# Softmax rows of three attentions: divided by their sums on GpSimd instead of on VectorE

## The reference

```python
x += W_out[ groupnorm(FoX heads) | groupnorm(MLA heads) | groupnorm(dilated-window heads) ]
x += memory cross-attention(rmsnorm(x), rmsnorm(mem))   # 4 heads, 256 memory tokens
x += top-4-of-32 clamped-SwiGLU experts(rmsnorm(x))
```

```python
p = jax.nn.softmax(s, axis=-1)      # exp(s - max) divided by its row sum
out = einsum("bhqk,bkhd->bqhd", p, v)
```

## Time and profile before

| what | value |
|---|---|
| median of 3 runs | 1135.68 us (1135.57 to 1135.76) |
| the profiled execution's own time | 1137.97 us |
| its span, first to last instruction | 1136.2 us |
| TensorE busy | 1091.2 us (96%) |
| VectorE busy | 316.2 us (28%) |
| ScalarE busy | 192.3 us (17%) |
| GpSimd busy | 136.2 us (12%) |
| mean DMA rate over the span | 378 GB/s |

### The profile page before, as it was taken

One profiled execution on the slowest core, in us unless ns is written; L12 is line 12 of the kernel. 1 busy time (PEld: TensorE's weight loads), 2 busy tenths in 40 slices (PEclk: granted clock), 3 DMA queues, 4 the chain that ended last, 5 costly groups with the idle time before them and its releaser, 6 DMA issues.

```text
span 1136.2 us, 13637 instructions
## 1 busy us (share of the span) xinstructions
PE 1091.2 (96%) x5069; PEld 442.7 (39%) x5069; DVE 316.2 (28%) x666; ACT 192.3 (17%) x389; POOL 136.2 (12%) x289
## 2 busy tenths in 40 slices
PE   7999999999999999999999999999999999999997
PEld 4666756633333333333333333333333333333332
DVE  4475754512222222222222222211211112222222
ACT  1144433311111111111111111111111111110111
POOL 1041300211111111111111111111111111111100
PEclk9999999899999999999999999999999999999999
DMA  6913368399999999999999999999999999999995
GB/s 228 358 38 149 126 241 333 153 389 428 426 429 427 427 429 429 427 430 427 429 427 430 428 427 430 427 429 427 430 428 427 431 427 429 427 430 427 428 430 239
DMA packets 44024, 429.06 MB, mean 378 GB/s; under 512 B 6336, under 2 KB 13792, under 8 KB 19168
## 3 DMA queue, kind: packets, MB, share of 16 engines
q1 hardware_dynamic: 43376, 427.67, 89.8%
q10 hardware_dynamic: 624, 1.07, 0.2%
HBM read 427.67 MB, written 1.05 MB: 377 GB/s over the span
## 4 chain that ended last, share of the span: by engine, by line
PE 66%; DMA 28%; DVE 4%; ACT 1%; issue 1%; ACTq 0%; DVEq 0%; SPq 0%
PE banks L705 27%; DMA ring<-in_w_e_dram 27%; PE banks L725 13%; PE banks L313 8%; PE banks L648 4%; PE banks L675 4%; PE banks L738 2%; PE banks L656 2%; PE banks L295 1%; PE banks L388 1%; PE banks L528 1%; PE banks L664 1%; DMA gain_rows<-in_g_ffn_dram 1%; PE banks L330 1%; PE banks L346 0%
## 5 line engine op out<-in xcount | busy, mean ns | idle before, releaser
L705 PE MATMUL banks<-ring,xg_T 128*64 128x512 f32 x2048 | 478.3, 599 | 24.4 <-DMA ring<-in_w_e_dram 23.2
L705 PEld LDWEIGHTS banks<-ring,xg_T 128*64 128x64 f32 x2048 | 135.8, 136 | 306.1 <-issue 254.3
L725 PE MATMUL banks<-ring,act_T 128*64 128x512 f32 x1024 | 232.9, 596 | 0.4 <-DVE act_T L1826 0.4
L1798 DVE TENSOR_TENSOR x_sb<-x_sb,banks 128x1024 f32<-128x1024 f32 x64 | 78.2, 1221 | 415.2 <-PE banks L675 382.6
L725 PEld LDWEIGHTS banks<-ring,act_T 128*64 128x64 f32 x1024 | 70.3, 137 | 132.5 <-issue 128.1
L1808 DVE TENSOR_TENSOR glu<-banks,b_T 128x512 f32<-128x512 f32 x32 | 22.1, 692 | 242.1 <-PE banks L738 242.1
L1033 POOL COPY picked<-slot_table 128x2 f32 (+1 forms) x32 | 6.0, 188 | 562.9 <-PE banks L664 562.9
L675 PE MATMUL banks<-y_sb,hot_gate_T 64*128 64x512 f32 x256 | 72.0, 640 | 0.8 <-ACT y_sb L1316 0.8
L1303 ACT COPY hidden<-banks 128x1024 f32<-128x1024 f32 x32 | 32.4, 1012 | 206.6 <-PE banks L705 206.6
L1289 ACT COPY xg_rows<-banks 128x512 f32<-128x512 f32 x33 | 19.3, 585 | 272.9 <-PE banks L648 272.9
L648 PE MATMUL banks<-h_sb,hot_slot 128*64 128x512 f32 x264 | 64.1, 607 | 0.5 <-DVE hot_slot L1766 0.5
(11 more groups left out here) (304 smaller groups left out, 777.5 us busy)
## 6 DMA issues: line engine op xcount, KB each, us to landing
ring<-in_w_e_dram SPq DMA_DIRECT2D x190, 2048.0 KB, 37.6
w_out_sb<-in_w_out_dram SPq DMA_DIRECT2D x1, 4096.0 KB, 13.3
ring<-in_w_e_dram SPq DMA_DIRECT2D x4, 1024.0 KB, 40.8
w_in_qk<-in_w_in_dram SPq DMA_DIRECT2D x1, 2048.0 KB, 14.8
w_mkv_sb<-in_w_mkv_dram SPq DMA_DIRECT2D x1, 2048.0 KB, 10.7
w_in_cq<-in_w_in_dram SPq DMA_DIRECT2D x2, 768.0 KB, 7.7
w_in_qc<-in_w_in_dram SPq DMA_DIRECT2D x1, 1536.0 KB, 17.0
w_in_kc<-in_w_in_dram SPq DMA_DIRECT2D x1, 1536.0 KB, 15.2
```

The source lines that it names most:

```text
L705: ins = TE.matmul(PS[SLOTS * h:SLOTS * h + SLOTS, B_W1 + b, :], left, ring[slot][:, 2 * F * j + F * h + 512 * b:2 * F * j + F * h + 512 * ...
L725: ins = TE.matmul(PS[SLOTS * h:SLOTS * h + SLOTS, B_W2, :], actT[:, c % 4, c // 4, :], ring[slot][:, D * j + 512 * h:D * j + 512 * h + 512 ...
L1798: V.tensor_tensor(X[:, t, :], X[:, t, :], PS[:, first:first + 2, :].rearrange("p b n -> p (b n)"), ALU.add).then_inc(S("added"), 1)
```

## The change

The multiplication of the probabilities moves from VectorE's list to GpSimd's. VectorE keeps the reciprocals (`invert_sums`) and counts a new semaphore `sums_inverted`, once for each unit. From the third unit on it waits first until the unit two before it has been scaled, since the reciprocals' columns are used again. GpSimd's `scale_probs` waits for the reciprocals and multiplies; it is called at six places of its list. TensorE's wait on `p_scaled` stays as it is.

```diff
         pool.wait_ge(S("rope_tables"), 1)
+        def scale_probs(*names):
+
+            for name in names:
+                u = U_OF[name]
+                c = 2 * (u % 2)
+                pool.wait_ge(S("sums_inverted"), u + 1)
+                G.tensor_scalar(Pb[:, u % 2, 0:P], Pb[:, u % 2, 0:P], rowinv[:, c:c + 1], None, ALU.mult)
+                G.tensor_scalar(Pb[:, u % 2, P:], Pb[:, u % 2, P:], rowinv[:, c + 1:c + 2], None,
+                                ALU.mult).then_inc(S("p_scaled"), 1)
+
...
         link(G.tensor_tensor(keys, keys, SG["g_kb"].unsqueeze(1).to_broadcast([P, 12, QK]), ALU.mult))
+        scale_probs("f0", "f1")
         for w in (1, 0):
             if w == 0:
+                scale_probs("f2", "f3")
                 pool.wait_ge(S("mla_q_normed"), 1)
...
+        scale_probs("m0", "m1", "m2", "m3")
         pool.wait_ge(S("dil_normed"), 1)
         pool.wait_ge(S("mla_rotated"), 1)
...
+        scale_probs("m4", "m5")
         pool.wait_ge(S("turned_out"), turned_no["gains"])
         pool.wait_ge(S("w_mq_in"), 16)
...
+        scale_probs("d0", "d1", "d2", "d3", "d4", "d5")
         pool.wait_ge(S("router_in"), 16)
...
-        def scale_probs(name):
+        def invert_sums(name):
             u = U_OF[name]
             c = 2 * (u % 2)
             dve.wait_ge(S("exped"), u + 1)
-            link(V.reciprocal(rowinv[:, c:c + 2], rowsum[:, 2 * (u % 4):2 * (u % 4) + 2]))
-            V.tensor_scalar(Pb[:, u % 2, 0:P], Pb[:, u % 2, 0:P], rowinv[:, c:c + 1], None, ALU.mult)
-            V.tensor_scalar(Pb[:, u % 2, P:], Pb[:, u % 2, P:], rowinv[:, c + 1:c + 2], None,
-                            ALU.mult).then_inc(S("p_scaled"), 1)
+            if u >= 2:
+                dve.wait_ge(S("p_scaled"), u - 1)
+            V.reciprocal(rowinv[:, c:c + 2], rowsum[:, 2 * (u % 4):2 * (u % 4) + 2]).then_inc(S("sums_inverted"), 1)
...
```

More of the change, by code:

```diff
@@ L1595, in _ @@
         gain_heads(QKb[:, 0], SG["g_qb"], MLA_H, QK).then_inc(S("mla_q_normed"), 1)
-        scale_probs("f0")
-        scale_probs("f1")
+        invert_sums("f0")
+        invert_sums("f1")
         project("qc", 1)
@@ L1608, in _ @@
         values(0)
-        scale_probs("f2")
-        scale_probs("f3")
+        invert_sums("f2")
+        invert_sums("f3")
         project("kc", 1)
@@ L1618, in _ @@
                   cols_of(0, "dil").rearrange("p (t h) -> p t h", t=NT))
-        scale_probs("m0")
-        scale_probs("m1")
+        invert_sums("m0")
+        invert_sums("m1")
         project("vc", 0)
@@ L1626, in _ @@
         scale_heads(dil, y, 12, HD)
-        scale_probs("m2")
-        scale_probs("m3")
+        invert_sums("m2")
+        invert_sums("m3")
         gain_heads(dil[:, :, 0:6], SG["g_qc"], 6, HD)
@@ L1634, in _ @@
         score("m5")
-        scale_probs("m4")
-        scale_probs("m5")
+        invert_sums("m4")
+        invert_sums("m5")
         group_roots("f", 256)
@@ L1652, in _ @@
         score("d1")
-        scale_probs("d0")
-        scale_probs("d1")
+        invert_sums("d0")
+        invert_sums("d1")
         memory("mem_v", 0, 256)
@@ L1660, in _ @@
         gain_heads(kv, gk[:], MEM_H, HD).then_inc(S("mem_keys_normed"), 1)
-        scale_probs("d2")
-        scale_probs("d3")
+        invert_sums("d2")
+        invert_sums("d3")
         memory("mem_v", 1, 256)
@@ L1667, in _ @@
         score("d5")
-        scale_probs("d4")
-        scale_probs("d5")
+        invert_sums("d4")
+        invert_sums("d5")
         add_group("f", 1, 0)
```

## The result

The changed kernel took **1150.6 us** (median of four runs, 1149.5 to 1152.8) against 1135.7 us for the kernel before in the same session. The ratio is 1.0118, with a 95% interval of 1.0101 to 1.0135, so the change costs **13.4 us** (11.5 to 15.3); the two medians lie 14.9 us apart. The forecast was 1141.9 us, 6.2 over before, with a range of 1136.0 to 1149.5: the sign was right, the size was less than half of what came, and the measured time lies above the range.

What follows compares the result with a forecast made beforehand. The weight stream bounds the expert stage, so attention losses reach the end whole: 2.4 + 1.4 + 1.0 + 1.4 = 6.2 us over the median of 1135.68 gave 1141.9 us, range 1136.0 to 1149.5.

Steps and rivals of the forecast that it cites:

- The stream: Expert stage: the weight stream fills the DMA engines, so a microsecond lost or won in attention arrives at the end whole.
- m0/m1: Pair m0/m1: scaled at 111.65 us, so the next scores start at 112.1 instead of 111.11, cost 1.0 us.
- m2/m3: Pair m2/m3: two gain products meet three of the four scalings, next scores start at 121.6 us, cost 1.4 us.
- GpSimd's own queue: Rotations and w_mq product behind GpSimd's scalings: hidden, key/query rotations with 1.4 us or more to spare.
- the f pairs: Pair f0/f1 and the way to the next projection, which begins at 95.8 us instead of 93.48: cost 2.4 us.
- the d pairs: Among the other four pairs: covered by a projection or merge, cost nothing; d2/d3 the tightest, 2.4 + 0.16 us just fit.
- The clock: Projection after f0/f1: TensorE's idling lowers its clock, a second loss costing 1.4 us; the present one stays.
- the price of a scaling: GpSimd: 0.46 us for 128 columns and 0.75 for 256, 1.2 us a unit, 2.4 a pair, from two-input products.
- The collisions: GpSimd beside VectorE's two-input products: each of the two products holds up one scaling.
- The cheap case: GpSimd scales as cheaply as its selects, 1.4 us a pair: +0.7 us, 1136.4, no difference; chance 0.15.
- The dear case: Scaling costs like the two-operation rows, 4.0 us a pair: +15.5 us, 1151.2; everything above +9 counted here; chance 0.20.
- The faster case: VectorE's relief keeps TensorE's clock up at the second kc projection: -2.4 us, 1133.3; chance 0.05.

Runs made afterwards that it cites:

- products moved to m3: Changed kernel with VectorE's list in another order, and the dilated heads' two gain products put behind the eviction of vc1: 1139.5 us, ratio 1.0025.
- only f: Changed kernel with only f0 to f3 scaled on GpSimd, VectorE keeping the m and d units: 1142.3 us, ratio 1.0060.
- products at f2: Changed kernel with VectorE's two products of the memory rows moved behind the reciprocals of f2/f3: 1149.7 us, ratio 1.0105.
- products out of both: Changed kernel with the two products of the memory rows moved behind the stretch of the f pairs, after `dil_ready`: 1145.5 us, ratio 1.0067.
- kept busy: Changed kernel with 28 idle identity matmuls on TensorE ahead of f0's transposes: 1148.5 us, ratio 1.0087.
- only m: Changed kernel with only m0 to m5 scaled on GpSimd, VectorE keeping the f and d units: 1143.4 us, ratio 1.0042.
- only d: Changed kernel with only d0 to d5 scaled on GpSimd, VectorE keeping the f and m units: 1138.1 us, ratio 1.0012.
- changed in the other order: Changed kernel with f reciprocals ahead of VectorE's mla query products and kc eviction, memory products after `dil_ready`: 1139.5 us, ratio 1.0022.
- reordered kernel: Kernel before, scaling on VectorE, with f scalings ahead of mla query products and kc eviction, memory products after `dil_ready`: 1131.2 us, ratio 0.9947.
- split kernel: Changed kernel in its own order, GpSimd scaling only the first query tile's 128 columns and VectorE the second's 256: 1137.5 us, ratio 1.0004.

## Why the prediction came out too low

**What held.** The stream: the start of the expert stage came 11.46 us later and the end 11.46 later. The sign, and the places: f0 to f3, m0/m1, m2/m3. GpSimd's own queue cost nothing: the second set of rotations ended at 103.6 us and TensorE asked for them at 105.2. The memory and dilated rotations, the loads and the 11 us of freed VectorE time changed nothing either.

**Term by term.** Without the clock, the f pairs cost 3.9 us (forecast 2.4, which by its own numbers is 2.3), m0/m1 1.7 (1.0), m2/m3 2.2 (1.4) and the d pairs 0.9 (0). The clock's net cost between the two traces is 2.5 (1.4). Another 0.3 stands ahead of the change's first wait. These are the 11.5 us of the traces. The step that failed most is the price of a scaling, which is in all four terms of the pairs; after it comes the clock.

**The price, put at 1.2 us a unit, is 1.48.** I took the line through the two-input products, because they too have "one arithmetic operation a column". The scaling alone takes 0.60 and 0.92 us where that line gave 0.46 and 0.75. It lies in the interval of the bounds (0.7 to 2.0), and my choice within it was too low by 0.55 us a pair. This makes m0/m1 dearer, and the f2/f3 pair, 0.9 where I saw little; d0/d1 and d2/d3 cost 0.9 instead of 0 ("2.4 + 0.16 us just fit", and 2.95 does not); and it is a part of m2/m3's 2.2 instead of 1.4. At f0/f1 it is 0.55 of the 0.8 us by which f1's delay of 3.0 exceeds the forecast's 2.2.

**The collisions: the mechanism was right, its rule was not.** I had each product hold one scaling, as four rotations of the earlier trace rows seemed to say. What the runs show is one scaling held over all products that VectorE issues back to back, and then most of its own time after the last: the wide one ended 0.71 us after two products (changed kernel) and 0.70 (products moved to m3), the narrow one 0.38 (moved to f2) and 0.39 (m2). The Trainium skill's "SBUF — State Buffer", section "Who interferes with whom", says that the second to issue blocks fully. For the first of two products the trace agrees: the scaling was issued 0.17 us behind it. For the second it doesn't, since that one came behind the scaling, and the scaling still waited for its end. I had read my rule off rotations, and those do fare otherwise: in the earlier trace rows one rotation ended while the second product of L1602 still ran, and the two products took 2.76 us instead of 2.35. So a rotation gets in between two products and a scaling did not, in any of the four cases. Whether the number of inputs makes that difference wasn't tried. The wrong rule cost the forecast little, some 0.3 us at f0/f1. Moving the products moved the hold in two kernels (to f2, to m3), since a pair occupies GpSimd for 2.95 us; only products put behind the whole stretch of the pairs, as in the kernel of 1145.5 us, held nothing there.

**The clock was sized by one row.** I took one loss of 1.4 us, and "the present one stays". The profile has 2.3 us behind f0/f1 (also the transposes and scores ran slow, not only the projection), 1.7 us behind m2/m3 that I had not foreseen at all, and 1.5 less at kc1. I had built a term of the sum, and the rival that gained by it, on a row of one execution, and the traces together show how little one execution says. The waits in one stretch of TensorE's list, and the traces in which the granted clock fell behind them or stayed at 1.00:

| waits | fell | stayed |
|---|---|---|
| 3.65 to 3.69, then 0.58 to 0.85 | changed, only f (f0/f1); products at f2 | |
| 1.71 or 1.72, then 0.93 or 0.94 | products out of both (f0/f1 and f2/f3); kept busy (f2/f3) | changed, only f (f2/f3); products at f2 (f0/f1) |
| 1.45 | before | only m, only d |
| 1.02 or 1.03, then 0.93 (m2/m3) | changed, only m, products out of both | products at f2, kept busy, changed in the other order |

And there is a loss with no wait ahead of it, as the profile counts busy time. In the router's stretch, just before the expert stage, every kernel has the same code. Before and then only d, same columns as in the earlier trace rows:

```profile
206.00:212.00 6.00, 6.00 (x37) 4.28 (x36) 3.23 (x8) 2.80 (x7) 2.20 (x1) 1.00 0.36 90
212.00:218.00 6.00, 6.00 (x32) 5.96 (x31) 3.84 (x23) 0.00 (x0) 0.15 (x1) 0.55 1.01 431
...
204.00:220.00 16.00, 14.04 (x107) 11.37 (x107) 10.57 (x46) 6.27 (x14) 4.72 (x2) 1.00 0.53 200
```

From the query projection of L528 to the expert stage it takes 42.8 us in five traces (before, changed, only m, and the changed kernel in the other order, with and without the moved gains), 41.5 to 41.8 in three and 40.2 in four. That is up to 2.7 us between two traces which is no matter of the edits. The two traces compared above both have it, so their 11.5 us stand. The medians lie 3.4 us further apart than the traces, because the trace of before is 2.3 us above its median and that of the changed kernel 1.2 below its own; kc1's loss of 1.5 is a part of the former.

**The rivals.** The cheap case is refuted: the ratio of the scalings to VectorE's of the earlier trace rows is 0.60 to 0.334 and 0.92 to 0.377. The page of the Trainium skill that I set against my price, "GPSIMD Engine Reference", section 4.1 (one-input work roughly at line rate), does not hold for this instruction here: between 128 and 256 columns it takes 2.5 ns a column. The dear case, "everything above +9 us", holds the number, but not as I had told it: at 2.95 us a pair and not 4.0, with the clock making the difference. The faster case did not occur. Its idea, that TensorE gains if the f pairs are ready sooner, was right, and the reordered kernel drew 6.0 us from it with VectorE, not GpSimd, doing the scaling.

**What stays open.** What decides whether the granted clock falls: equal waits differ in it, and it also falls where the profile has TensorE busy without a break. Also, why the kernel of 1145.5 us is faster than the changed one by more than its trace shows.

## What to carry to other kernels

An engine that is 28% busy is not short of time; what mattered was the order of its list in the 20 us where TensorE waited for it. Ask first what stands between the input and the result that the bounding engine waits for, and move that, before moving work to a slower engine: here the one gave 6 us, the other lost 13. When an elementwise step is on a path, the slower engine's time for a **pair** in flight counts, not its busy share; here, two-input products of VectorE near it in time came on top. A wait that follows from it on TensorE may cost again in clock; before a term is built on a lowered clock, look whether a second execution shows it, and before two traces are compared, look whether stretches with the same code took the same time.

## What the runs showed of the hardware

- A one-operation TENSOR_SCALAR on GpSimd with float32 in SBUF took 0.60 us for 128 columns and 0.92 for 256 in every kernel here when alone, so about 0.28 us fixed and 2.5 ns a column; VectorE's same instructions are 0.334 and 0.377.
- A scaling held on GpSimd waited, in all four cases looked at, for the end of both of VectorE's two-input products. VectorE wasn't slowed by it: two products of 1024 columns took 2.35 us with a scaling held behind them and 2.36 with nothing beside them. Beside rotations, which are two-input products on GpSimd themselves, they took 2.76, and 2.75 in the split kernel.
- The same waits (1.71 and 0.93 us) in front of the same projection were followed by a granted clock of 1.00 in one kernel and of 0.50 in another. In the three kernels in the other order, whose waits at the f pairs were under 1 us, no lowered clock showed between 80 and 132 us; it didn't in the split kernel either, with waits of 1.0 and 1.1 us there.
- The granted clock also fell to 0.50 after 6 us in which the profile has TensorE busy throughout (router's stretch of the kernel before), and in four other traces the same code ran at 1.00 throughout.
